# Differential attention: GpSimd alone scales and adds the second map, ScalarE makes three of four copies

## What is computed

```python
def diff_attention(q, k, v, lam_vecs, subln, rel_bias, lam_init):
    ...
    def block(args):
        ...
        sc = jnp.einsum('bqhmd,bkhmd->bmhqk', qb, k) * scale + bias[None, None]
        p = jax.nn.softmax(sc, axis=-1)
        a = p[:, 0] - lam * p[:, 1]
        return jnp.einsum('bhqk,bkhd->bqhd', a.astype(v.dtype), v)
```

## Time and profile before

| | |
|---|---|
| median of 3 runs | 4055.61 us (4053.83 to 4058.95) |
| span of the profiled execution | 4058.1 us |
| TensorE busy | 3793.6 us (93%) |
| VectorE busy | 2243.3 us (55%) |
| ScalarE busy | 1659.8 us (41%) |
| GpSimd busy | 2463.3 us (61%) |
| differential stage | about 1183 to 1697 us, and again in layer 1 |

### The profile page before, as it was taken

The page is one execution under the profiler, slowest core; times in us unless marked ns, Lnnn a source line. Parts: engine busy times, 40 slices in busy tenths (PEclk is TensorE's granted clock), DMA queues, the critical chain, the costliest instruction groups (busy, mean ns, idle before and its releaser), DMA issues. The chain is left out here.

```text
span 4058.1 us, 51537 instructions
## 1 busy us (share of the span) xinstructions
PE 3793.6 (93%) x19002; PEld 2623.3 (65%) x19002; DVE 2243.3 (55%) x3973; ACT 1659.8 (41%) x2886; POOL 2463.3 (61%) x1381
## 2 busy tenths in 40 slices
PE   8999999999989899889989999999999889998898
PEld 7789774555545666557777897755555456665577
DVE  3002125555569999875530030255555699998755
ACT  3112103333348888761031021033333588887610
POOL 1221326877769999855512213267777699997555
PEclk9999999999999999999999999999999999999999
DMA  5433535233320222235353334422333202223353
GB/s 177 127 130 121 145 129 124 60 92 74 78 59 1 57 57 58 66 104 187 135 177 122 133 114 142 140 68 55 72 72 72 59 1 57 57 58 71 105 179 135
DMA packets 180864, 392.43 MB, mean 97 GB/s; under 512 B 18014, under 2 KB 100168, under 8 KB 168968
## 3 DMA queue, kind: packets, MB, share of 16 engines
q1 hardware_dynamic: 179752, 387.75, 34.1%
q10 hardware_dynamic: 864, 1.41, 0.2%
HBM read 255.93 MB, written 135.67 MB: 96 GB/s over the span
## 5 line engine op out<-in xcount | busy, mean ns | idle before, releaser
L1297 POOL TENSOR_TENSOR mla_sum_pool<-mla_sum_pool,mla_probs 128x1024 f32<-128x1024 f32 (+1 forms) x336 | 777.6, 2314 | 209.4 <-ACT mla_probs L1258 184.4
L1315 DVE TENSOR_REDUCE carry_row_max<-psum 128x1 f32<-128x512 f32 x688 | 474.5, 690 | 415.7 <-PE psum L1130 410.7
L1258 ACT ACTIVATE mla_probs<-psum 128x1024 f32<-128x1024 f32 x384 | 373.3, 1021 | 693.8 <-PE psum L1167 686.6
L1613 ACT ACTIVATE diff_probs<-psum,diff_shift 128x1024 f32<-128x1024 f32 x512 | 566.5, 1112 | 186.2 <-DVE diff_shift L1697 180.5
L1690 DVE TENSOR_REDUCE diff_row_max<-psum 128x1 f32<-128x1024 f32 x512 | 611.6, 1218 | 44.5 <-PE psum L1534 37.5
L1560 PE MATMUL psum<-ident,diff_probs 128*128 128x128 f32 x2048 | 328.3, 284 | 104.3 <-DVE diff_turned L1724 66.9
L638 PE MATMUL psum<-in_x_hi,in_w_hi 128*128 128x512 f32 x1024 | 409.9, 400 | 2.7 <-ACT in_mla_val L745 2.7
L638 PE MATMUL psum<-in_x_hi,in_w_lo 128*128 128x512 f32 x1024 | 405.8, 396 | 0.0
L638 PE MATMUL psum<-carry_firsts,in_w_hi 128*128 128x512 f32 x1024 | 404.6, 395 | 0.0
L1560 PEld LDWEIGHTS psum<-ident,diff_probs 128*128 128x128 f32 x2048 | 215.9, 141 | 280.1 <-issue 178.2
L1180 PE MATMUL psum<-mla_probs,mla_v_op 128*64 128x512 f32 x1536 | 374.8, 609 | 0.0
(11 more groups left out here) (213 smaller groups left out, 7408.7 us busy)
## 6 DMA issues: line engine op xcount, KB each, us to landing
in_w_raw<-in_w_in SPq DMA_DIRECT2D x64, 512.0 KB, 3.9
split_d<-in_out SPq DMA_DIRECT2D x64, 512.0 KB, 2.7
raw_d<-in_out SPq DMA_DIRECT2D x32, 512.0 KB, 2.6
mq_d<-in_out SPq DMA_DIRECT2D x48, 256.0 KB, 3.6
mk_d<-in_out SPq DMA_DIRECT2D x48, 256.0 KB, 3.9
carry_firsts<-split_d SPq DMA_DIRECT2D x48, 256.0 KB, 8.0
carry_weights<-split_d SPq DMA_DIRECT2D x48, 256.0 KB, 7.7
carry_weights<-split_d SPq DMA_DIRECT2D x16, 768.0 KB, 18.0
```

The source lines that it names most:

```text
L1258: nc.scalar.activation(probs[:, s % RING, :].rearrange("p (a n) -> p a n", n=CH), psum[:, S0 + 2 * (s % 2):S0 + 2 * (s % 2) + 2, :], ACT.E ...
L1297: nc.gpsimd.tensor_tensor(acc, start, probs[:, s % RING, mine], ALU.add).then_inc(pool_added, 1)
L1315: nc.vector.tensor_reduce(row_max[:, u % 2, qb, n:n + 1], psum[:, sweep_bank(g), :], AX.X, ALU.max).then_inc(maxed, 1)
L1613: nc.scalar.activation(dst[:, half * HALF:(half + 1) * HALF].rearrange("p (a n) -> p a n", n=CH), banks(n, m, half), ACT.Exp, bias=shift[: ...
```

## The change

GpSimd takes over the whole scaling of the second map, in both halves, with `tensor_scalar`: one tensor operand, times the ratio (one value a row), times 1.0. ScalarE no longer scales; instead it makes copy 2 of each unit, which VectorE made before, between the two halves of the second map's exponential. VectorE keeps copy 0 alone. The counts of the two copy semaphores follow. The window stage's row scaling on GpSimd gets the same form of instruction.

```diff
         def copies(n, c):
-            return (act_copied if c % 2 else dve_copied), 2 * n + c // 2 + 1
+            return (act_copied, 3 * n + c) if c else (dve_copied, n + 1)
...
                         nc.scalar.activation(dst[:, half * HALF:(half + 1) * HALF].rearrange("p (a n) -> p a n", n=CH),
                                              banks(n, m, half), ACT.Exp, bias=shift[:, n % 2, m:m + 1], scale=DIFF_SCALE,
                                              accum_out=row_sum[:, n % 2, m, half:half + 1]).then_inc(exped, 1)
-
-                def scale(n):
-                    act.wait_ge(ratio_ready, n + 1)
-                    at = 0 if n < LATE else HALF
-                    first = probs1[:, n % DEEP1, at:at + CH]
-                    nc.scalar.activation(first, first, ACT.Copy, scale=ratio[:, n % 2:n % 2 + 1]).then_inc(act_scaled, 1)
+                        if m == 1 and half == 0:
+                            copy(n - LAG, 2)
...
                     copy(n - LAG - 1, 3)
                     if on:
                         exp(n, 0)
-                    if n == UNITS:
-                        scale(n - 1)
                     copy(n - LAG, 1)
-                    if 1 <= n < UNITS:
-                        scale(n - 1)
                     if n % 2:
                         odd_half((n - 5) // 2)
                     if on:
                         exp(n, 1)
+                    else:
+                        copy(n - LAG, 2)
...
                     pool.wait_ge(ratio_ready, n + 1)
-                    at = 0 if n < LATE else HALF
                     done = 2 * n if n < LATE else LATE + n
-                    second = probs1[:, n % DEEP1, at + CH:at + HALF]
-                    nc.gpsimd.tensor_tensor(second, second, ratio[:, n % 2:n % 2 + 1].broadcast_to([P, HALF - CH]),
-                                            ALU.mult).then_inc(times_ratio, 1)
-                    pool.wait_ge(act_scaled, n + 1)
-                    pool.wait_ge(times_ratio, done + 1)
-                    nc.gpsimd.tensor_tensor(probs[:, n % DEEP, at:at + HALF], probs[:, n % DEEP, at:at + HALF],
-                                            probs1[:, n % DEEP1, at:at + HALF], ALU.add).then_inc(mixed, 1)
...
+                    halves = (0, HALF) if n < LATE else (HALF,)
+                    for k, at in enumerate(halves):
+                        part = probs1[:, n % DEEP1, at:at + HALF]
+                        nc.gpsimd.tensor_scalar(part, part, ratio[:, n % 2:n % 2 + 1], 1.0, ALU.mult, ALU.mult
+                                                ).then_inc(times_ratio, 1)
+                        pool.wait_ge(times_ratio, done + k + 1)
+                        nc.gpsimd.tensor_tensor(probs[:, n % DEEP, at:at + HALF], probs[:, n % DEEP, at:at + HALF], part,
+                                                ALU.add).then_inc(mixed, 1)
...
                 for n in range(UNITS + DRAIN + 2):
                     on = n < UNITS
-                    copy(n - LAG - 1, 2)
...
                         row = probs[:, qb % DEEP, h, 0:w]
-                        nc.gpsimd.tensor_tensor(row, row, inv[:, qb % 2, h:h + 1].broadcast_to([P, w]), ALU.mult
+                        nc.gpsimd.tensor_scalar(row, row, inv[:, qb % 2, h:h + 1], 1.0, ALU.mult, ALU.mult
                                                 ).then_inc(scaled, 1)
```

More of the change, by code:

```diff
@@ L1438, in diff_attention @@
             sem(n) for n in ("scored", "maxed", "shifted", "exped", "summed", "inverted", "ratio_ready"))
-        act_scaled, times_ratio, mixed, turn_done, pv_done, odd_out, o_ready = (
-            sem(n) for n in ("act_scaled", "times_ratio", "mixed", "turn_done", "pv_done", "odd_out", "o_ready"))
+        times_ratio, mixed, turn_done, pv_done, odd_out, o_ready = (
+            sem(n) for n in ("times_ratio", "mixed", "turn_done", "pv_done", "odd_out", "o_ready"))
         dve_copied, act_copied, dve_mixed = sem("dve_copied"), sem("act_copied"), sem("dve_mixed")
         def copies(n, c):
-            return (act_copied if c % 2 else dve_copied), 2 * n + c // 2 + 1
+            return (act_copied, 3 * n + c) if c else (dve_copied, n + 1)
         def turn_bank(n, c):
```

## The result

| | median, us | runs |
|---|---|---|
| before | 4056.7 | 4053.8 to 4059.0 |
| changed | 4146.8 | 4145.7 to 4151.3 |
| ratio | 1.0228 | 95% interval 1.0215 to 1.0241 |

The account below looks back on a forecast made before the run. GpSimd was taken to bound the differential stage at 7.83 us a unit; the new loop's 120 x 0.77 = 92, ends +2 and window stage -2 gave 92, so 4150, or 4148 on the median's footing; range 4095 to 4205.

Parts of the forecast that it names:

- What bounds the kernel now: Differential stage: GpSimd sets the pace at 7.83 us a unit, which the other three engines only just hold.
- the loop under it: Differential stage, TensorE, VectorE and ScalarE: 3.91 + 4.08 = 7.99 us with the band in the second half.
- The new loop: Differential stage, through ScalarE's copy 2: 8.35, 8.74 or 8.96 us by block, mean 8.60 against 7.83, 92 us in all.
- GpSimd's price: Differential stage: tensor_scalar over 1024 columns at the cast's 1.04 us, upper bound 1.90; 6.96 or 8.68 us a unit.
- The window stage: L1918, six GpSimd multiplies a block over 384 columns: cheaper only in a layer's uncovered last block, -1 us a layer.
- B: Differential stage: the loop doesn't bind, the shift comes earlier; mean 7.6 us a unit, -25 us, 4030; chance 7%.
- C: GpSimd in the differential stage: tensor_scalar dearer than the two-operand multiply; at 2.4 us, +222 us, 4278; chance 4%.
- D: TensorE in the differential stage: idle 1.3 us each unit, granted clock falls; about +1 us a unit, 4270; chance 7%.
- What would show it: Trace signs: GpSimd idle before tensor_scalar; TensorE's transpose waits led by ScalarE's copy, some 1.3 us, over 100; ratios 8.3 to 9.0 apart.

## Why the prediction was right

**What bounds the kernel now.** Right, and it needed both halves. GpSimd's 7.83 us a unit was the pace, and the loop under it 7.73, measured with GpSimd relieved. A reader who had stopped at "GpSimd is 97% busy" would have forecast 3975 for its relief.

**The new loop.** From the earlier trace rows the sum was 8.74 us, measured 8.74 in a block shown above; for the first half of the keys 8.35 against 8.38; for blocks cut in two pieces 8.96 against 8.85 to 8.90. The 8.74 was too long for three of the seven units that it stood for: two round the middle of a head and one at its end take 8.54 to 8.62. In the first half the shift comes 2.00 us after S(0, second), as forecast, and VectorE's order from there took 4.16 instead of 4.07 (1327.96 to 1332.12), since T(0) did hold the first copy. Over a full head all this makes 8.57 against the 8.60 of the sum. The 60 units of a layer average 8.61 and 8.59, because the first few of a layer are longer, one of them 9.95 us; that 8.60 fits these so closely is in part luck. 120 x 0.77 = 92 us; the two layers show 516.8 - 470.0 and 515.3 - 469.7, 92.5 in sum. The times differ by 90.0, the profiled spans by 85.7. From the first ratio of a layer to its last the changed kernel takes 94 us more in the two layers together; the rest of its profiled execution is 8 us shorter, nearly 6 of them between the last ratio of layer 0 and the first of layer 1. That stretch takes 1527 to 1534 us in the traces of all the kernels here, with the change and without it, so this looks like scatter between executions and not like an effect of the change.

**GpSimd's price.** 1.04 us was taken, from the cast; it is 1.12. The range to 1.90 was right to be called harmless: the two-operand price was run and moved the time by about 5 us, where the text gave 0.1 us a unit, 12 at most. With the hand-over GpSimd's own work is 2 x 2.34 + 2 x 1.21 = 7.10 us a unit, where the sum had 6.96; it waits for the ratio either way.

**The window stage.** GpSimd's rows of 384 columns take 0.59 us instead of 0.83. Between the first instruction on the window's probabilities and the last a layer takes 117.6 to 119.8 us in the three kernels with the old multiply, mean 118.6, and 117.4 to 119.1 in the nine with the new one, mean 117.9. That fits the 1 us a layer that was set for it, but the ranges overlap; it isn't shown.

**The rivals.** B (the loop doesn't bind) fell: with the band in the second half the exponential starts 2.60 us after the second map's scores, before and after, and with it in the first half 2.56 before and 2.59 after; VectorE's relief didn't reach it. Its picture of what would remain, a mean of 7.6 us, was near: with the copy given back it is 7.73. C was wrong for this form, but it names a real mechanism: with the one-factor form GpSimd sets the pace at 10.5 us. D didn't happen with one pause of 1.3 us a unit (clock 1.00 from 1216 to 1746 us), and did in the two kernels with longer or more pauses: 2.28 us and more once a unit, and some 1.6 us at most up to twice a unit. The page that spoke for D (the Trainium skill, TensorE: Matmul & The Clock Gate, "A second HAM failure mode: psum-queue depth-cycling") is borne out by these two kernels and not by the changed one. The rule of the Trainium skill, GPSIMD Engine Reference, section 4.1, that one-input operations run near line rate, fits the cast (1.04 us) and the two-factor form (1.12), which take less than half of an add's 2.38, and not the one-factor form (2.85); here the measurement decides.

**What would show it.** One sign was misjudged: TensorE's waits were to be led by ScalarE's copy, and for its matmuls they are (74.6 us in one layer, 58 times), but the weight loads' largest line names GpSimd, whose add was over 0.68 us before the load shown began. A releaser inferred by time has to be tested when the engine named is idle itself.

## What to carry to other kernels

When the busiest engine is to be relieved, measure first the loop that lies under it: here it was 0.1 us of 7.8 away, and the relief was worth 16 us of an apparent 83. A copy between two halves of a long instruction is cheap in the engine's sum and dear on the path, if another engine waits for it: price the place, by what must come ahead of it in the queue, and not the load. In a loop of scores, maximum and exponential, issue the part with additional matmuls first; that alone took 26 us off the kernel with the copy given back, and 18 off the changed one.

## What was not expected of the hardware

On GpSimd, tensor_scalar over 128x1024 in float32 takes 1.12 us with two factors and 2.85 us with one, the same operand and destination. TensorE's granted clock fell to 0.50 within a stage that was busy otherwise: of 118 pauses of 2.28 us and more 47 were followed by transposes at the lower clock, and 71 of the same lengths weren't. With pauses of some 1.6 us at most, up to twice a unit, the clock fell seven times in a layer's stage, and with one of 1.3 us a unit not at all in the middle of the stage. The mean granted clock of the profiled execution was 0.961, 0.975 and 0.982 in the three.
